# Stick-breaking attention of a decoder step: mask and subtraction on VectorE, magnitude on ScalarE, no tile work on GpSimd

## What is computed

```python
def stick_breaking(q, k, v, q_pos, k_pos, bias):
    z = jnp.einsum('bqhd,bkhd->bhqk', q, k).astype(jnp.float32) * (q.shape[-1] ** -0.5)
    z = z + bias.astype(jnp.float32)[None, :, None, None]
    causal = k_pos[None, :] < q_pos[:, None]
    log_1mb = jnp.where(causal, -jax.nn.softplus(z), 0.0)
    suffix = lax.cumsum(log_1mb, axis=3, reverse=True)
    log_a = -jax.nn.softplus(-z) + suffix - log_1mb
    a = jnp.where(causal, jnp.exp(log_a), 0.0)
    return jnp.einsum('bhqk,bkhd->bqhd', a.astype(v.dtype), v)
```

## Time and profile before

| | us |
|---|---|
| median of 3 runs | 2341.76 |
| lowest and highest run | 2339.83, 2342.63 |
| profiled execution, its time | 2341.29 |
| profiled execution, its span | 2339.7 |
| TensorE busy | 1979.1 (85%) |
| VectorE busy | 1173.8 (50%) |
| ScalarE busy | 855.4 (37%) |
| GpSimd busy | 281.2 (12%) |

### The profile page before, as it was taken

How to read it: one execution, slowest core, us unless ns; L and a number is a source line. 1 busy time by engine, 2 the same in 40 slices (tenths; PEclk the granted TensorE clock), 3 DMA queues, 4 the chain that set the end, 5 groups by cost and what they waited for, 6 DMA issues and landing times. The chain is left out here.

```text
span 2339.7 us, 27599 instructions
## 1 busy us (share of the span) xinstructions
PE 1979.1 (85%) x10140; PEld 1528.1 (65%) x10140; DVE 1173.8 (50%) x1355; ACT 855.4 (37%) x1171; POOL 281.2 (12%) x356
## 2 busy tenths in 40 slices
PE   5999999698898799991488992599999999997598
PEld 5999999687777667770286541466666666664485
DVE  5121212188888645443342224466666666664664
ACT  4111111166666334440031000444444444442454
POOL 0110101143333200001021003000000000000210
PEclk7999999899999969895689995799999999999699
DMA  3444343434121222207244003999999999993520
GB/s 110 116 132 120 108 126 113 140 114 145 46 73 46 58 51 41 41 1 196 72 156 145 28 18 140 340 373 354 352 363 350 345 352 355 359 350 148 199 99 37
DMA packets 222237, 392.70 MB, mean 168 GB/s; under 512 B 29467, under 2 KB 100619, under 8 KB 222164
## 3 DMA queue, kind: packets, MB, share of 16 engines
q1 hardware_dynamic: 202916, 325.28, 40.9%
q0 software_dynamic: 14928, 50.60, 6.8%
q10 hardware_dynamic: 4320, 15.85, 1.7%
HBM read 321.02 MB, written 78.35 MB: 171 GB/s over the span
## 5 line engine op out<-in xcount | busy, mean ns | idle before, releaser
L1825 PE MATMUL x_Y<-x_wd,x_hT 128*128 128x512 f32 x512 | 228.1, 598 | 32.4 <-DVE x_hT L1918 32.4
L86 PE MATMUL p_acc<-uh,p_wl 128*128 128x344 f32 x720 | 235.1, 327 | 12.8 <-DVE ul L292 8.6
L88 PE MATMUL p_acc<-uh,p_wh 128*128 128x344 f32 x720 | 230.7, 320 | 0.0
L87 PE MATMUL p_acc<-ul,p_wh 128*128 128x344 f32 x720 | 230.6, 320 | 0.0
L304 DVE COPY p_zk<-p_tp 128x512 f32<-128x512 f32 (+1 forms) x90 | 44.2, 547 | 304.5 <-PE p_tp L225 304.5
L1825 PEld LDWEIGHTS x_Y<-x_wd,x_hT 128*128 128x128 f32 x512 | 94.6, 190 | 147.0 <-issue 147.0
L1903 DVE TENSOR_TENSOR x_wgl<-x_wg,x_wgh 128x2048 fp32r<-128x2048 f32 x64 | 146.4, 2287 | 69.7 <-ACT x_wgh L1856 69.7
L268 ACT ACTIVATE p_zc<-p_acc 128x344 f32<-128x344 f32 x90 | 41.2, 458 | 321.7 <-PE p_acc L88 321.7
L86 PEld LDWEIGHTS p_acc<-uh,p_wl 128*128 128x128 f32 x720 | 135.9, 189 | 17.8 <-issue 15.0
L1903 DVE TENSOR_TENSOR x_wul<-x_wu,x_wuh 128x2048 fp32r<-128x2048 f32 x64 | 143.6, 2285 | 0.0
L544 PE MATMUL g_acc<-uh,g_wl 128*128 128x344 f32 x384 | 131.8, 343 | 9.1 <-ACT u L575 7.0
(11 more groups left out here) (317 smaller groups left out, 4062.0 us busy)
## 6 DMA issues: line engine op xcount, KB each, us to landing
x_wg<-in_w_gate SPq DMA_DIRECT2D x64, 1024.0 KB, 7.2
x_wu<-in_w_up SPq DMA_DIRECT2D x64, 1024.0 KB, 7.1
x_wd<-in_w_down SPq DMA_DIRECT2D x32, 2048.0 KB, 12.1
x_x<-xs SPq DMA_DIRECT2D x32, 512.0 KB, 9.8
ys<-x_y POOLq DMA_DIRECT2D x32, 512.0 KB, 5.5
zT<-p_zc ACTq DMA_DIRECT2D x30, 516.0 KB, 3.5
p_w<-in_w_in SPq DMA_DIRECT2D x30, 512.0 KB, 5.5
ztok<-p_zk POOLq DMA_DIRECT2D x30, 512.0 KB, 4.6
```

The costliest lines, as they stand in the source:

```text
L86: pe.matmul(out, w_low, m_high, start=first, stop=False)
L87: pe.matmul(out, w_high, m_low, start=False, stop=False)
L88: return pe.matmul(out, w_high, m_high, start=False, stop=last)
L1825: last = pe.matmul(Y[c][:, :], hT[:, k, :], wd[:, b, k, c * 512:(c + 1) * 512], start=(k == 0), stop=(k == KF - 1))
```

## The change

GpSimd's loop is gone; it still builds the mask tile once. VectorE does the mask at the start of a step, ahead of the scan, and the subtraction after the maximum, ahead of the copies. The magnitude is an activation on ScalarE in front of the exponential. What VectorE's sign-bit operation waited for (the mask, a free `w` buffer) ScalarE waits for now.

```diff
@@ -596,6 +596,9 @@
                 if live(s, EXP):
                     u = s - EXP
                     n = (unit(u)[2] + 1) * P
+                    act.wait_ge(masked, u + 1)
+                    need(act, al_full, u - WB + 1)
+                    act.activation(w[:, u % WB, 0:n], z[:, u % ZB, 0:n], ACT.Abs).then_inc(w_full, 1)
                     act.wait_ge(w_full, u + 1)
                     act.activation(w[:, u % WB, 0:n], w[:, u % WB, 0:n], ACT.Exp, scale=-1.0).then_inc(e_full, 1)
                     act.wait_ge(e_full, u + 1)
@@ -617,19 +620,6 @@
             pool.affine_select(out=causal[:, :], in_=causal[:, :], compare_op=ALU.is_gt, fill=NEG, base=0,
                                pattern=[[-1, P]], channel_multiplier=1).then_inc(const, 1)
             pool.wait_ge(const, 2)
-            for s in range(LAST + 1):
-                if live(s, FOLD):
-                    u = s - FOLD
-                    i = unit(u)[2]
-                    pool.wait_ge(z_full, scaled(u) + 1)
-                    diag = z[:, u % ZB, i * P:(i + 1) * P]
-                    pool.tensor_tensor(diag, diag, causal[:, :], ALU.add).then_inc(masked, 1)
-                if live(s, SCAN):
-                    u = s - SCAN
-                    n = (unit(u)[2] + 1) * P
-                    pool.wait_ge(cum_full, u + 1)
-                    pool.tensor_tensor(z[:, u % ZB, 0:n], z[:, u % ZB, 0:n], w[:, u % WB, 0:n],
-                                       ALU.subtract).then_inc(al_full, 1)
 
         @block.vector
         def _(dve):
@@ -642,6 +632,14 @@
                 for c in range(CH):
                     if cut_at[c] == s:
                         cut(c)
+                if live(s, FOLD):
+                    u = s - FOLD
+                    i = unit(u)[2]
+                    if u == 0:
+                        dve.wait_ge(const, 2)
+                    dve.wait_ge(z_full, scaled(u) + 1)
+                    diag = z[:, u % ZB, i * P:(i + 1) * P]
+                    dve.tensor_tensor(diag, diag, causal[:, :], ALU.add).then_inc(masked, 1)
                 if live(s, SCAN):
                     u = s - SCAN
                     n = (unit(u)[2] + 1) * P
@@ -653,11 +651,14 @@
                     u = s - FOLD
                     n = (unit(u)[2] + 1) * P
                     dve.wait_ge(masked, u + 1)
-                    need(dve, al_full, u - WB + 1)
                     need(dve, cum_full, u - 1)
-                    dve.tensor_scalar(w[:, u % WB, 0:n].bitcast(I32), z[:, u % ZB, 0:n].bitcast(I32),
-                                      0x7FFFFFFF, None, ALU.bitwise_and).then_inc(w_full, 1)
                     dve.tensor_scalar(r[:, u % 2, 0:n], z[:, u % ZB, 0:n], 0.0, None, ALU.max).then_inc(r_full, 1)
+                if live(s, SCAN):
+                    u = s - SCAN
+                    n = (unit(u)[2] + 1) * P
+                    dve.wait_ge(cum_full, u + 1)
+                    dve.tensor_tensor(z[:, u % ZB, 0:n], z[:, u % ZB, 0:n], w[:, u % WB, 0:n],
+                                      ALU.subtract).then_inc(al_full, 1)
                 if live(s, TURN):
                     u = s - TURN
                     need(dve, o_full, u // 2)
```

## The result

The changed kernel takes 2335.55 us (median of 18 runs, 2330.7 to 2344.4), the kernel before 2346.94 us in the same session (18 runs, 2339.8 to 2365.8). The ratio is 0.9945 with a 95% interval of 0.9925 to 0.9964: the change saves 11.4 us by the medians (8 to 18 by the interval), where 29 were forecast. The profiled execution took 2332.7 us, with a span of 2331.0.

What follows compares the result with a forecast made beforehand. VectorE and TensorE were both near full, TensorE waiting for VectorE's copies. Gains of 24 us (copies) and 7 (clock) less 2 (fill) made 29, so 2341.3 - 29 = 2312 us, TensorE becoming the limit; range 2298 to 2330.

Steps and rivals of the forecast that it cites:

- The wait for the copies: Stick-breaking stage: TensorE's wait for VectorE's copies of the transposed weights was to fall from 34.6 to about 11 us.
- The clock: TensorE's granted clock in the stick-breaking stage was to rise to 0.98 as waits go, returning 7 us.
- The 2 us for the fill: First units of the stick-breaking stage: ScalarE's longer chain, covered by nothing there, was to cost 2 us.
- It has cover: ScalarE stands 84.6 us for scores.: ScalarE in the stick-breaking stage: the magnitude's added 43.6 us was to fit into 84.6 us of standing for scores.
- ScalarE's wait for scores: Sign in the stick-breaking stage: this wait was to fall by roughly 44 us and the stage's shortening.
- TensorE's 4.6 us a step to ScalarE's 3.9: Work per step (one unit of one head and 128 queries) after the change: TensorE 4.6 us becomes the limit, ScalarE 3.9.
- The sum's largest term: VectorE's work sum: the sign-bit mask of line 658 leaves VectorE, -105.3 us, all of it ahead of the copies.
- The rival that ScalarE's chain takes over: ScalarE's magnitude, exponential and logarithm in a row delay VectorE's scan, +10 us after cuts; 2325 us, chance 0.20.
- another stage moving by more than 2 us: Sign against the forecast: if any stage other than stick-breaking moves by more than 2 us, it is wrong.
- The range's low bound: Whole kernel: the forecast case's lowest end was 2296 us (all TensorE waits and the clock, 45 us); the range began at 2298.
- In steps with a cut ... 6 x 1.8 = 11 us stay: Gate-weight cuts after the fill: 12, half ahead of value products, leave 11 us of TensorE's 34.6 us copy wait.
- The mask's wait: Rival: the mask ahead of VectorE's scan holds it in 16 steps, deciding from 3.6 us; 2350 us, chance 0.05.

## Why the prediction was wrong

**Right.** VectorE and TensorE were both near full, and VectorE's copies were what TensorE stood for. GpSimd's neighbourhood made line 658 dear: 1645 ns with it, 460 without. The maximum, the subtraction, the mask and the magnitude cost 460, 751, 283 and 681 ns, each within 5 ns of its term. The wait for the copies fell to 12.1 us (forecast about 11). The clock gave some 6 to 7 us: the forecast says 7, though its own 24/34.6 of 11 makes 7.6. The 2 us for the fill are not confirmed: the first scan came 0.9 to 1.6 us late, and that was made up by the ninth.

**The step that failed** is the one on ScalarE: "It has cover: ScalarE stands 84.6 us for scores." From that the sum took nothing for 43.6 us of new work. The total of an in-order engine's idle time is not cover for what stands behind the new work in a busy step. The magnitude sits ahead of the eviction, the next gate sum needs the eviction, and the 7.0 us of the earlier trace rows were the sign that this hand-over was already late at times; the prediction read that row and left it as it was. It became 16.4 us. The runs give the price of the step: without the magnitude on ScalarE the stage is 7.6 us shorter, with evictions ahead of it 6.3, with a second magnitude 26.8 longer. ScalarE's wait for scores, which was to fall by 44 us and the stage's shortening, fell by 28.5; the rest of the new work came out of ScalarE's other waits. The ratio of TensorE's 4.6 us a step to ScalarE's 3.9 hid it, since those are means: in the step shown at 546 us ScalarE's work runs to 4.1 us without a gap before the eviction ends.

With the 9.4 us in it the stage's sum would have been 29 - 9.4 = 19.6 us, against 14.6 measured. Of the 5.0 us left, 1.5 are the copies' share (22.5 against 24), 3.3 the part of that wait which only changed its name to issue, and 0.3 the clock. This split holds as far as the account does: the 3.3 are a reading, and the remainder of 1.9 is set against the forecast's 2 for the fill without having been measured. The two experiments give 6.3 to 7.6 us for the magnitude's place, so 7 to 8 of the 14.4 us that are missing rest on the account alone.

The sum's largest term, 105.3 us for the magnitude leaving VectorE, also had its credit in the wrong place. The relief was GpSimd's leaving: with the magnitude kept on VectorE it costs 29.5 us there, and the stage is 22.2 us shorter than before, against 14.6 with it moved. That choice was not among the rivals.

**The rival that ScalarE's chain takes over** (2325 us, 0.20) had the engine and about the price: 10 us, where 9.4 were lost, and its stage would be 16 us shorter against 14.6. That the two sums lie so close is partly luck: the rival has 24 us for the copies, where the account has 19.2, and 4 for the clock, where it has 6.7. It had the wrong link: through exponential and logarithm to VectorE's scan. That wait is 4.5 us after the change. The rule of the Trainium skill cited there, "ScalarE: Activation LUTs", "Rules for kernel authors", which names operations such as maximum and add and not the magnitude, fits these runs once GpSimd is empty: the magnitude on VectorE gives a stage of 344.4 us, on ScalarE 352.0. With GpSimd busy it is the other way (366.6 and 360.8). I gave it too little, because I set it against step means.

**The measured time lies above that rival too**, and above the range. Of the 23.6 us between 2312 and 2335.55, 5.6 lie in the starting point (one execution, below the median of 18 runs) and 17.6 are missing gain. The stage's 14.6 us alone would give 2341.3 - 14.6 = 2326.7 us. The rest up to the profiled 2332.7 is the dilated stage, which varies by more than that between executions of one program. The prediction said that another stage moving by more than 2 us would make it wrong; it should have given that stage's own spread a place in the range. The range's low bound is also off by its own words: all TensorE waits and the clock make more than 45 us, as the 7.0 us for evictions are not in it. Against the runs of the same session the change is 11.4 us, and the interval of the ratio, 8 to 18 us, holds the stage's 14.6 and excludes the 29.

**"In steps with a cut ... 6 x 1.8 = 11 us stay"** gave the right size by luck. The 1.8 us a cut stand in no row (the instance worked out there has 2.3), and later cuts left the copies' wait at 11.2 us.

**The mask's wait**, the rival for slower, is there with 20.7 us in 10 places, longest 3.9, close to the 3.6 us from which it was to decide. Moving the mask behind the scan gave 2.8 us of stage and left 9.1 us of the wait, since it mostly falls where VectorE had slack.

**Why the second half of the gain was there after all.** With evictions, cuts and mask in their better places the stage is 337.6 us, 29.0 shorter than before. That equals the forecast sum by coincidence, as it takes three more edits than the change has.

## What to carry to other kernels

When work moves to an engine that idles, look up what that engine does behind the new work in its busiest steps, and who waits for it; a short existing wait there (7.0 us in 8 places) was the first to grow here, whatever the engine's total idle time. When a small operation takes longer than a large one, look for a neighbour that it waits for. Remove the neighbour, since removing the operation handed most of its wait to the next one (65.1 of 105.3 us). And test the parts of such a change apart: here emptying GpSimd gave 22.2 us, and the magnitude's move took 7.6 of them back. After the limit moves, repeat the cheap reorderings that were worth nothing before it moved: the early eviction was worth at most 1 us before this change and 6 after it.

## What the runs showed of the hardware that was not expected

The time of a stage that no edit touched varied by more than most edits are worth. At the start of the dilated stage TensorE waits some 18 us for a transfer (in the trace of before, 18.14 us up to 823.43, for the values), and the clock granted afterwards is at the lower level, 1.2 GHz (0.50 in the rows below). It stays there for different lengths. The kernel before in its first profiled execution, and the same kernel with early evictions, each in windows of 12 us (same columns as above). The windows are counted from 13.5 us behind the first memset of the slopes; the first two, at 0.50 in both, are not shown. First execution:

```profile
847.30:859.30 12.00, 12.00 (x40) 8.91 (x39) 5.78 (x9) 4.60 (x10) 0.00 (x0) 0.50 0.00 1
859.30:871.30 12.00, 11.69 (x64) 8.54 (x63) 5.95 (x8) 5.36 (x8) 0.00 (x0) 0.98 0.00 0
871.30:883.30 12.00, 11.38 (x89) 10.14 (x89) 5.33 (x10) 6.80 (x14) 0.00 (x0) 1.00 0.01 1
```

With early evictions:

```profile
846.00:858.00 12.00, 12.00 (x41) 8.92 (x39) 5.90 (x8) 4.13 (x7) 0.00 (x0) 0.50 0.01 1
858.00:870.00 12.00, 12.00 (x38) 8.49 (x37) 4.36 (x7) 3.49 (x7) 0.00 (x0) 0.50 0.00 0
870.00:882.00 12.00, 12.00 (x36) 8.36 (x35) 2.95 (x6) 2.74 (x5) 0.00 (x0) 0.50 0.00 0
882.00:894.00 12.00, 12.00 (x57) 10.91 (x56) 4.79 (x10) 5.26 (x10) 0.00 (x0) 0.51 0.01 1
894.00:906.00 12.00, 11.69 (x87) 10.14 (x86) 3.14 (x8) 4.81 (x12) 0.00 (x0) 1.00 0.00 0
```

TensorE's busy time, which is modelled, fills these windows or nearly so, and its code here is the same. In the first the clock is back after three windows at 0.50, in the second after five and a sixth at 0.51. A later drop in the same stage varies as well: the kernel before spent one window at 0.50 there in one execution and two in the other. The dilated stage takes 243.2 and 249.9 us in the two executions of the kernel before and 265.1 with early evictions, and 243.0 to 266.0 over all kernels run. What decides how long the lower clock lasts stayed open; that the same program gave 243.2 and 249.9 shows that it need not be the kernel. Whether the edits make the long cases (264.5 to 266.0, seen in three of the kernels) more frequent is not shown, as each has one trace. It is also why the comparison by stage was needed: a median of 6 or 18 runs carries this spread. The early evictions in the kernel before take 0.4% longer with a stage that is no longer than before, and its dilated stage is the likely place.
